# First head of a gated DeltaNet trunk: k's projection, convolution and Silu put ahead of v's, with one semaphore per convolution

## The reference, cut to what matters

```
mod = silu(cond) @ ada_w + ada_b                       # adaLN: shift, scale, gate
h = rmsnorm(x, norm1_g) * (1 + scale1) + shift1
proj = h @ w_in                                        # pool, q, k, v, gate, beta, alpha, merge columns
qkv = silu(short_conv(proj[..., OFF_Q:OFF_G], conv_w)) # 5 taps, each channel by itself
q = l2norm(q) * DN_HEAD_DIM ** -0.5 ; k = l2norm(k)    # 8 heads of 128
g = -exp(a_log) * softplus(alpha + dt_bias)            # log decay
o_f, s_f = gated_delta_chunked(q, k, v, beta, g, s0_f) # and the same from the other end
```

## Time and profile before

| what | value |
|---|---|
| median of 3 runs | 2406.78 us |
| lowest and highest run | 2404.05 and 2406.78 us |
| span of the profiled execution | 2402.9 us (its own time is not listed beside the runs) |
| TensorE matmul busy | 2305.9 us, 96% |
| VectorE, ScalarE, POOL busy | 46%, 39%, 16% |
| granted clock of TensorE | full in all of 40 slices but the first and one near 1600 us |

### The profile page before, as it was taken

One profiled execution on the slowest core, in us unless ns is written; L12 is line 12 of the kernel. 1 busy time (PEld: TensorE's weight loads), 2 busy tenths in 40 slices (PEclk: granted clock), 3 DMA queues, 4 the chain that ended last, 5 costly groups with the idle time before them and its releaser, 6 DMA issues.

```text
span 2402.9 us, 39720 instructions
## 1 busy us (share of the span) xinstructions
PE 2305.9 (96%) x14208; PEld 1684.5 (70%) x14208; DVE 1107.6 (46%) x2143; ACT 931.8 (39%) x2434; POOL 381.5 (16%) x270
## 2 busy tenths in 40 slices
PE   6989999999999999999999999869999999999997
PEld 3456666575656566665644444569999999999997
DVE  2587686868687776866245316730001000010003
ACT  3164646556373746555311223113222232222323
POOL 0241313223040413123100000001001010010101
PEclk8999999999999999999999999979999999999999
DMA  9521212020120212121343422368877888778885
GB/s 343 220 63 38 69 37 69 18 89 18 43 63 22 67 37 69 28 70 38 122 155 118 167 79 88 114 238 279 293 266 251 286 285 294 259 255 284 290 291 213
DMA packets 198883, 362.31 MB, mean 151 GB/s; under 512 B 9083, under 2 KB 72520, under 8 KB 195724
## 3 DMA queue, kind: packets, MB, share of 16 engines
q1 hardware_dynamic: 192267, 341.83, 40.7%
q0 software_dynamic: 6528, 19.47, 3.1%
HBM read 320.63 MB, written 40.65 MB: 150 GB/s over the span
## 4 chain that ended last, share of the span: by engine, by line
PE 85%; DVE 5%; issue 3%; ACT 3%; DMA 2%; DVEq 0%; SPq 0%; ACTq 0%; POOLq 0%; POOL 0%
PE bank L755 22%; PE bank L2447 21%; PE bank L2461 11%; PE bank L2060 5%; PE bank L1797 5%; PE bank L963 3%; PE bank L1815 2%; PE bank L733 2%; PE bank L955 2%; PE bank L1021 2%; PE bank L741 1%; PE bank L1032 1%; PE bank L1037 1%; DMA arena<-in_ada_w 1%; PE bank L1036 1%
## 5 line engine op out<-in xcount | busy, mean ns | idle before, releaser
L755 PE MATMUL bank<-arena 128*128 128x512 f32 x1344 | 675.4, 606 | 0.0
L2447 PE MATMUL bank<-arena 128*128 128x144 f32 x4096 | 513.0, 286 | 3.1 <-ACT arena L2481 3.1
L2447 PEld LDWEIGHTS bank<-arena 128*128 128x128 f32 x4096 | 509.7, 190 | 3.2 <-ACT arena L2481 3.2
L2554 DVE TENSOR_TENSOR arena<-arena,bank 128x144 f32<-128x144 f32 x128 | 39.1, 306 | 697.8 <-ACT arena L2495 697.8
L755 PEld LDWEIGHTS bank<-arena 128*128 128x128 f32 x1344 | 217.0, 191 | 88.9 <-issue 87.5
L2461 PE MATMUL bank<-arena 128*128 128x144 f32 x2048 | 257.3, 286 | 0.7 <-DVE arena L2554 0.7
L2461 PEld LDWEIGHTS bank<-arena 128*128 128x128 f32 x2048 | 253.8, 189 | 1.9 <-DVE arena L2554 0.9
L2495 ACT ACTIVATE arena<-bank 128x144 f32<-128x144 f32 x128 | 37.5, 293 | 460.5 <-PE bank L2447 460.5
L963 PEld LDWEIGHTS bank<-arena 128*128 128x128 f16 x1296 | 96.4, 98 | 156.3 <-issue 138.0
L1141 ACT ACTIVATE arena<-bank 128x384 f16<-128x384 f16 (+1 forms) x360 | 160.5, 491 | 92.0 <-PE bank L963 67.9
L795 ACT ACTIVATE arena<-bank 128x128 f32<-128x128 f32 (+1 forms) x156 | 75.9, 491 | 166.8 <-PE bank L755 107.7
(11 more groups left out here) (318 smaller groups left out, 3044.9 us busy)
## 6 DMA issues: line engine op xcount, KB each, us to landing
arena<-in_exp_w_gate SPq DMA_DIRECT2D x32, 2048.0 KB, 9.9
arena<-in_exp_w_up SPq DMA_DIRECT2D x32, 2048.0 KB, 14.9
arena<-in_exp_w_down SPq DMA_DIRECT2D x32, 2048.0 KB, 10.7
arena<-in_w_in SPq DMA_DIRECT2D x52, 512.0 KB, 5.3
arena<-in_ada_w SPq DMA_DIRECT2D x24, 1024.0 KB, 7.8
side_dram<-arena SPq DMA_DIRECT2D x20, 576.0 KB, 4.2
arena<-g_dram SPq DMA_DIRECT2D x16, 576.0 KB, 4.2
arena<-in_x_sample SPq DMA_DIRECT2D x16, 512.0 KB, 7.4
```

The costliest lines, as they stand in the source:

```text
L755: ins = nc.tensor.matmul(bank[:, 0:LH], w[:, k, :], x[:, k, :], start=(k == 0 and job[2] in "127"), stop=(k == KH - 1), skip_group_check=( ...
L2447: last = nc.tensor.matmul(banks[3 + f % 2][:, m * CAP:(m + 1) * CAP], w_unit[2 * half + m][:, k, col:col + P], xsT[:, k, :], start=(k == 0 ...
```

## The change

- The last two prologue units swap: k2 is the eighth, v2 the ninth. ScalarE's copies of them swap too: k2's comes before the exponentials of the decays (`act_decays`), v2's behind them.
- The 15 taps of head 0 are taken in the order q, k, v.
- Instead of `conv_done` each convolution has its own semaphore, and `silu(j)` waits for its own to reach h + 1. A wait for v's is added ahead of `evac("start")`, since those copies write the rows that v's convolution reads.
- The weights of head 1 are loaded in the order q, k, v: the load in `sync3` is k's, the one in `sync4` v's.
- Two later semaphores are merged with earlier ones (`rstd2` into `x_rstd`, `xn_ready2` into `xn_ready`, with their counts raised by NT), so that the total number of semaphores does not grow.

```
-            sp.wait_ge(sem("pj_filled"), FIRST.index("v2") + 1)
-            load_w(sp, 1, 2)
+            sp.wait_ge(sem("pj_filled"), FIRST.index("k2") + 1)
+            load_w(sp, 1, 1)
...
-        FIRST = ("q0", "q1", "v0", "v1", "k0", "k1", "q2", "v2", "k2")
+        FIRST = ("q0", "q1", "v0", "v1", "k0", "k1", "q2", "k2", "v2")
...
-        CONV_TURN_FIRST = (3, 0, 2, 1)
+        CONV_DONE = ("q_conv_done", "k_conv_done", "v_conv_done")
+        CONV_TURN_FIRST = (3, 0, 1, 2)
...
             sp.wait_ge(sem("pj_filled"), len(FIRST))
-            load_w(sp, 1, 1)
+            load_w(sp, 1, 2)
...
             def silu(j):
-                act.wait_ge(sem("conv_done"), 3 * h + CONV_TURN.index(j))
+                act.wait_ge(sem(CONV_DONE[j]), h + 1)
...
             silu(0)
+            act.wait_ge(sem(CONV_DONE[2]), h + 1)
             if not last_h:
                 evac("start")
...
-            ins.then_inc(sem("tap_done" if tap < TAPS - 1 else "conv_done"), 1)
+            ins.then_inc(sem("tap_done" if tap < TAPS - 1 else CONV_DONE[j]), 1)
...
-            evacs("v2")
-            act_decays(act)
             evacs("k2")
+            act_decays(act)
+            evacs("v2")
...
-            taps = [(j, tap) for j in (0, 2, 1) for tap in range(TAPS)]
+            taps = [(j, tap) for j in (0, 1, 2) for tap in range(TAPS)]
...
-            pe.wait_ge(sem("xn_ready2"), i + 1)
+            pe.wait_ge(sem("xn_ready"), NT + i + 1)
...
-                dve.wait_ge(sem("rstd2"), i - 1)
+                dve.wait_ge(sem("x_rstd"), NT + i - 1)
```

More of the change, by code:

```diff
@@ L1594, in prologue_act @@
             act_softplus(act)
+            evacs("k2")
+            act_decays(act)
             evacs("v2")
-            act_decays(act)
-            evacs("k2")
         def prologue_dve(dve):
@@ L2041, in sync7 @@
             sp.dma_start(x2_dram[t * P:(t + 1) * P, :], x_t[i % XR]).then_inc(sem(f"tile_out{i % XR}"), 16)
-            sp.wait_ge(sem("xn_ready2"), i + 1)
+            sp.wait_ge(sem("xn_ready"), NT + i + 1)
             sp.dma_start(xn_dram[t * P:(t + 1) * P, :], xn_t[i % XR]).then_inc(sem(f"tile_out{i % XR}"), 16)
@@ L2157, in act7 @@
             act.wait_ge(sem("act_step"), ACT_PRO + 2 * i + 2)
-            nc.scalar.activation(rstd[i % 2], lnb[i % 2], ACT.Exp, scale=-0.5).then_inc(sem("rstd2"), 1)
-            act.wait_ge(sem("rstd2"), i + 1)
+            nc.scalar.activation(rstd[i % 2], lnb[i % 2], ACT.Exp, scale=-0.5).then_inc(sem("x_rstd"), 1)
+            act.wait_ge(sem("x_rstd"), NT + i + 1)
             if i >= XR:
@@ L2162, in act7 @@
                 act.wait_ge(sem("h2T_filled"), i - 1)
-            nc.scalar.activation(xn_t[s], x_t[s], ACT.Copy, scale=rstd[i % 2]).then_inc(sem("xn_ready2"), 1)
+            nc.scalar.activation(xn_t[s], x_t[s], ACT.Copy, scale=rstd[i % 2]).then_inc(sem("xn_ready"), 1)
             if i == NL2:
@@ L2632, in factors @@
         act.wait_ge(sem("act_step"), act_ends[0])
-        nc.scalar.activation(frs[:, at:to], fln[:, at:to], ACT.Exp, scale=-0.5).then_inc(sem("rstd2"), 1)
+        nc.scalar.activation(frs[:, at:to], fln[:, at:to], ACT.Exp, scale=-0.5).then_inc(sem("x_rstd"), 1)
     def sync10(sp):
@@ L2658, in act10 @@
         act.wait_ge(sem("act_step"), act_ends[0])
-        nc.scalar.activation(last_rs[:, 0:1], last_ln[:, 0:1], ACT.Exp, scale=-0.5).then_inc(sem("rstd2"), 1)
+        nc.scalar.activation(last_rs[:, 0:1], last_ln[:, 0:1], ACT.Exp, scale=-0.5).then_inc(sem("x_rstd"), 1)
         act.wait_ge(sem("x_summed"), 1 + N_VECTOR_SQUARES + 2)
@@ L2665, in act10 @@
         act.wait_ge(sem("act_step"), act_ends[0])
-        nc.scalar.activation(last_rs[0:QROWS, 1:2], last_ln[0:QROWS, 1:2], ACT.Exp, scale=-0.5).then_inc(sem("rstd2"), 1)
+        nc.scalar.activation(last_rs[0:QROWS, 1:2], last_ln[0:QROWS, 1:2], ACT.Exp, scale=-0.5).then_inc(sem("x_rstd"), 1)
     def dve10(dve):
@@ L2670, in dve10 @@
         for n, (at, to) in enumerate(LAST_GROUPS):
-            dve.wait_ge(sem("rstd2"), NT + n + 1)
+            dve.wait_ge(sem("x_rstd"), NT + NT + n + 1)
             for t in range(at, to):
@@ L2681, in dve10 @@
         nc.vector.scalar_tensor_tensor(x_c[0:QROWS, :], banks[7][0:QROWS, 0:QD], gates_c[0:QROWS, E - 1:E], x_c[0:QROWS, :], ALU.mult, ALU.add).then_inc(sem("x_summed"), 1)
-        dve.wait_ge(sem("rstd2"), NT + len(LAST_GROUPS) + 1)
+        dve.wait_ge(sem("x_rstd"), NT + NT + len(LAST_GROUPS) + 1)
         nc.vector.scalar_tensor_tensor(x_l, x_l, last_rs[:, 0:1], fin_row, ALU.mult, ALU.mult).then_inc(sem("yf_ready"), 1)
-        dve.wait_ge(sem("rstd2"), NT + len(LAST_GROUPS) + 2)
+        dve.wait_ge(sem("x_rstd"), NT + NT + len(LAST_GROUPS) + 2)
         nc.vector.scalar_tensor_tensor(x_c[0:QROWS, :], x_c[0:QROWS, :], last_rs[0:QROWS, 1:2], fin_quarter[0:QROWS, :], ALU.mult, ALU.mult).then_inc(sem("yf_ready"), 1)
```

## The result

| | before | the changed kernel |
|---|---|---|
| median, 21 runs each | 2405.88 us | 2410.02 us |
| lowest and highest | 2403.96 and 2407.58 us | 2405.83 and 2411.01 us |
| ratio of the runs, 95% interval | | 1.0016 [1.0009, 1.0022] |
| span of the profiled execution | 2402.9 us | 2404.1 us |

The change costs 4.1 us, 0.16%. The forecast was 3.8 us, 2410.6 us in all, within 2404.5 to 2413.5, and slower by less than 0.2%. It came out as forecast.

A forecast was written before the change was run, and what follows sets the result against it. TensorE, holding 85% of the chain that ended last, was taken as the bound. L940 +4.1 us including slow clock, less about 0.3 before L955, gave +3.8 on 2406.8: 2410.6 us, range 2404.5 to 2413.5.

The forecast's parts named there:

- The wait for v's weights: First head, before TensorE's second job qvc1: TensorE idles 6.3 us until v's weights land at 131.7.
- The clock: After that gap TensorE resumes at 1.2 GHz, so qvc1 takes 3.74 us; charged 1.8 us, bounds 0 and 1.9.
- the row near 1560: Profile row cited as evidence: in a 5.62 us gap ending at 1562.18 the granted clock fell to 0.50.
- The sum: First head on TensorE: k turned (L940) at 144.1 against 140.02, +4.1 us; +3.8 us in all.
- worked without a gap for 8.72 us: TensorE's stretch from L926's start to the end of the piece before k's turn, 129.91 to 138.63, added after the wait.
- One small thing comes back, the 0.28 us before L955: First head: TensorE's 0.28 us idle before L955 should vanish, as VectorE has that much less to catch up.
- VectorE becomes the bound: Rival: first head, k's multiplications wait for POOL's sums, or v's weights land later; 0.7 to 4.7 us on top; chance 0.15.
- The gain was at most zero by this chain: Sentence in rival "Nothing moves" (2406.8 us, chance 0.14): the squares advanced in the first head were not what ended last.

The follow-up runs named there:

- The loads alone: The kernel before with only head 1's two loads swapped, k's in the first slot, v's in the second; median 2409.30 us, ratio 1.0017.
- the loads undone: The changed kernel with head 1's weights loaded in the old order, v's in the first slot, k's in the second; median 2404.29 us, ratio 0.9996.
- the run with the filler: The changed kernel plus 7 unread 128x512 matmuls on TensorE between prologue and head; median 2405.65 us, ratio 1.0000.
- the sums behind all masks: The changed kernel, both loads first, decays waiting only for their rows, five POOL sums of head 0 after all masks, qv7 awaiting its sum; 2405.88 us, ratio 1.0000.
- both loads in time: The changed kernel with v's, then k's weights for head 1 both loaded in the first slot; median 2405.10 us, ratio 1.0000.
- held back until the decays: The changed kernel, both loads first, decays waiting only for their rows, five POOL sums of head 0 after VectorE's 18 subtractions; 2405.84 us, ratio 1.0002.
- the semaphores alone: The changed kernel with every order put back, leaving only the new and merged semaphores and the added wait; median 2405.22 us, ratio 0.9998.

## Why the prediction was right, and where it was off

**The wait for v's weights** was the step that decided, and it held: 6.3 us forecast, 6.22 found, landing 7.3 us after the issue where 7.4 was taken. The loads alone give the slowdown (+0.17%), and with the loads undone it is gone.

**The clock** was charged at 1.8 us between bounds of 0 and 1.9. The gap brought it down, as the row near 1560 had said. Against the run with the filler it cost 1.1 us in the changed kernel's trace and 2.1 us in the other with the same gap, so 1.8 is fair, but the upper bound was too low: slow work lasted 2.8 us in the one and 4.4 us in the other, where I had taken 3.8 from one row. The reason given was weaker than the result: it went by the length of the gap, 2.59 us without and 5.62 us with a fall, and with the loads undone the clock fell after 2.42 us. The Trainium skill's page "TensorE: Matmul & The Clock Gate", section "What's actually happening", advises against fitting a count of cold matmuls and counts the ramp as under 1% of a span. Its remark that the count varies from run to run agrees with these two traces; leaving the ramp out would have missed 1.1 of 2.8 us in the one and 2.1 of 3.7 us in the other.

**The sum was too high for this trace and right for the median.** From the head's start L941 was forecast at 144.1 - 123.6 = 20.5 us and came at 141.79 - 122.21 = 19.6. Half of the difference is the shorter slow stretch. The other half is a mistake in "worked without a gap for 8.72 us": the first and the last start are 8.2 us apart (133.58 to 141.79); the last group's modelled end lies 0.3 us behind the start of what can follow it, and one of the starts in it had waited 0.2 us for ScalarE. The term to take is start to start.

**"One small thing comes back, the 0.28 us before L955"** was wrong: 0.24 us still stand there. VectorE did not get ahead: its second nine subtractions took 2.56 us instead of 1.85 with POOL's seventh sum beside them, and it ended at 143.4, just as v's first tiles were turned. But that is not why the wait stayed. With the sums behind all masks VectorE was ahead, and stood 0.53 us idle for TensorE's L940, and 0.25 us still stood before L955. From the start of L940 to that of L955 it takes 9.8 to 9.9 us in all three traces, so the small wait moves with k's turn.

**The rival "VectorE becomes the bound"** did not decide, but came closer than I said: k was normed at 140.7, and TensorE was free for it at 141.8. The two multiplications did not wait for a sum (0.29 and 1.22 us, as before): POOL was between its sixth and seventh, as forecast, for all but their last 0.4 us; the first nine subtractions did lengthen by 1.1 us, which I had left at 6.53.

**"The gain was at most zero by this chain"** was put as one sentence of a rival, and the runs bear it out as to the time: with both loads in time the heads' stretch is 1084.12 against 1084.07 us. By the chain alone it was not quite zero: k was turned 1.0 us earlier there, and the slow clock took that back.

**Size.** The traces show +2.8 us for the changed kernel and +3.7 for the loads alone, the medians +4.1 and +3.4. That the forecast of +3.8 came so near to the medians' +4.1 is in part luck, since the interval of that difference runs from 2.2 to 5.3 us. The slow clock behind the gap differs by 1 us between executions; that the rest of the medians' +4.1 comes from there too was not shown, since only one execution of each has a trace.

## What to carry to other kernels

When the production order of three things is changed, walk every queue that carries their successors: here the loads followed the new order in which their places came free, and the order in which the next head wants them stayed the old one. A wait that ends last on the path may still be worth nothing; before it is removed, read when the next two inputs of the same consumer arrive, and which engines must not run beside each other. And if a gap cannot be closed, its price on TensorE is the gap plus what runs at half clock behind it.

## What the runs showed of the hardware that was not expected

- **VectorE beside POOL.** Nine subtractions of 128x128 float32, SBUF to SBUF, took 1.85 us alone, and 5.50, 5.82, 6.53, 7.59 and 8.47 us the more POOL's work ran beside them (float32 sums, and in the last case one mask as well). An addition of two SBUF tiles (L1315) and predicated copies between SBUF tiles (L1320) were stretched too (1.48 to 4.14 and 2.90 to 3.96 us). An instruction that reads a bank and one SBUF tile was not (L1308, 2.88 and 2.88), and the two float16 copies (L1301) took 1.40 us beside POOL's sums, where those were held back until the decays, and 1.40 us beside its masks. The Trainium skill's page "SBUF — State Buffer", section "SBUF: two separate sides", says that the two engines share a port pair as an exclusive lock, held for a whole instruction, and that VectorE needs it in a faster mode of its own or with two inputs in SBUF. The trace agrees: in the worst case each of the seven stretched subtractions ended just behind the end of a POOL instruction, after 1.00 to 1.31 us instead of 0.28.
- **Moving POOL's sums never paid here.** The seven take it 9 to 11 us of the first head, and wherever they were put somebody waited: VectorE's subtractions beside them, its masks behind or beside them, or TensorE for the sums themselves. Behind each of these waits of 3.96 to 5.36 us TensorE also ran 5.5 to 6.1 us at half clock. Fewer sums in head 0, sums on another engine, a clock kept up by a filler, or the same move in the later heads, where 0.77 us stand before L955 each time, were not tried.
- **The clock fell with short waits too.** It fell in or just behind waits of 2.07, 2.42, 2.49, 3.09 and 3.47 us, and not behind the 2.59 us of the kernel before and of the semaphores alone.
- **A load issued too early holds its issuer.** Two loads behind four 1 MB ones took SyncE 6.81 us to issue, 6.32 of them for the second. A load by itself takes 0.4 us, and the second of two in the first slot, without the four right ahead of it, took 2.56. The stores, v's load and the decay rows behind them went out later; the state's request did not (2.74 us after the head's start, as before), since it waits for `scan_done`.
